# Second block of a two-block layer: pool products ahead of the gate branch's, gate branch kept in its banks, side taps by halves

## What is computed

```python
def second_block(x, meta_tokens, ...):
    h = concatenate([meta, x])
    u = rmsnorm(h, mix_norm_g)
    p = u @ w_in
    p_pool, p_bval, p_bgate, p_cgate, p_cx = split(p, [256, 256, 256, 512, 512])
    y_a = pool_mixer(p_pool, pool_w, pool_scale)        # running means of 2, 4, 8, 16, then a grouped product
    y_b = conformer_conv(p_bval, p_bgate, ...)          # 31 taps, layer norm, silu, product
    y_c = rglru_branch(p_cgate, p_cx, ...)              # 4 taps, gates, linear scan; gelu(p_cgate) * scan
    h = h + concatenate([y_a, y_b, y_c]) @ w_out
    u = rmsnorm(h, mlp_norm_g)
    h = h + square(relu(u @ w_up)) @ w_down
    return rmsnorm(h, final_norm_g)[16:]
```

## Time and profile before

| | us |
|---|---|
| median of 3 runs | 1053.14 (1053.1 to 1058.57) |
| the profiled execution | 1053.21 |
| its span | 1051.4 |
| PE busy | 1028.8 (98%) |
| DVE busy | 515.1 (49%) |
| ACT busy | 421.4 (40%) |
| POOL busy | 575.9 (55%) |

### The profile page before, as it was taken

How to read it: one execution, slowest core, us unless ns; L and a number is a source line. 1 busy time by engine, 2 the same in 40 slices (tenths; PEclk the granted TensorE clock), 3 DMA queues, 4 the chain that set the end, 5 groups by cost and what they waited for, 6 DMA issues and landing times.

```text
span 1051.4 us, 12703 instructions
## 1 busy us (share of the span) xinstructions
PE 1028.8 (98%) x5047; PEld 861.9 (82%) x5047; DVE 515.1 (49%) x835; ACT 421.4 (40%) x663; POOL 575.9 (55%) x712
## 2 busy tenths in 40 slices
PE   9999999999999999999999878999999999999997
PEld 7888888888888888888899766888788888888887
DVE  2781356665356633545677898457113213312323
ACT  5443445555624424443237663453213222212332
POOL 3655556556556764465634796464655544554551
PEclk9999999999999999999999999999999999999999
DMA  6323222122442215332222202322323232232212
GB/s 223 105 92 93 89 70 81 54 67 81 141 140 80 80 45 181 118 120 82 81 80 81 80 21 81 101 81 80 120 80 112 89 110 91 87 113 81 97 64 80
DMA packets 93500, 98.63 MB, mean 94 GB/s; under 512 B 3282, under 2 KB 88816, under 8 KB 93440
## 3 DMA queue, kind: packets, MB, share of 16 engines
q1 hardware_dynamic: 93440, 97.81, 28.7%
HBM read 95.71 MB, written 2.10 MB: 93 GB/s over the span
## 4 chain that ended last, share of the span: by engine, by line
PE 84%; DVE 11%; ACT 4%; issue 1%; DMA 1%; SPq 0%; DVEq 0%; ACTq 0%
PE ps L347 75%; DVE ps L1165 2%; PE ps L714 1%; PE ps L695 1%; PE ps L1623 1%; PE ps L839 1%; DVE Fm L1077 1%; DVE Hl L478 1%; PE ps L652 1%; PE ps L654 1%; DVE tmp L1589 1%; DVE Fm L1129 1%; DMA raw<-in_w_in 1%; DVE tmp L456 1%; DVE Al L1531 1%
## 5 line engine op out<-in xcount | busy, mean ns | idle before, releaser
L268 POOL TENSOR_TENSOR wlo<-raw,whi 128x256 fp32r<-128x256 f32 x668 | 509.4, 794 | 386.1 <-ACT whi L263 386.1
L347 PE MATMUL ps<-Hh,whi 128*128 128x512 f32 x832 | 330.0, 397 | 5.4 <-DVE Hl L1246 1.7
L347 PE MATMUL ps<-Hl,whi 128*128 128x512 f32 x832 | 325.4, 391 | 0.0
L263 ACT ACTIVATE whi<-raw 128x1024 fp32r<-128x1024 f32 x167 | 175.9, 1054 | 159.0 <-PE ps L347 152.7
L347 PE MATMUL ps<-Hh,wlo 128*128 128x512 f32 x832 | 209.1, 390 | 1.0 <-POOL wlo L268 1.0
L347 PE MATMUL ps<-Ah,whi 128*128 128x512 f32 (+1 forms) x576 | 197.7, 366 | 0.2 <-DVE Al L1531 0.2
L347 PE MATMUL ps<-Al,whi 128*128 128x512 f32 (+1 forms) x576 | 195.0, 361 | 0.0
L347 PEld LDWEIGHTS ps<-Hh,whi 128*128 128x128 f32 x832 | 156.9, 189 | 42.7 <-DVE Hl L408 4.2
L347 PEld LDWEIGHTS ps<-Hh,wlo 128*128 128x128 f32 x832 | 156.6, 188 | 34.2 <-POOL wlo L268 1.4
L347 PEld LDWEIGHTS ps<-Hl,whi 128*128 128x128 f32 x832 | 156.9, 189 | 31.8 <-issue 0.5
L347 PE MATMUL ps<-Ah,wlo 128*128 128x512 f32 (+1 forms) x576 | 125.2, 363 | 0.0
(11 more groups left out here) (291 smaller groups left out, 957.2 us busy)
## 6 DMA issues: line engine op xcount, KB each, us to landing
raw<-in_w_in SPq DMA_DIRECT2D x33, 1024.0 KB, 5.3
raw<-in_w_up SPq DMA_DIRECT2D x16, 1024.0 KB, 5.4
raw<-in_w_down SPq DMA_DIRECT2D x16, 1024.0 KB, 5.1
raw<-in_w_att_out SPq DMA_DIRECT2D x4, 1024.0 KB, 5.2
raw<-in_w_sg_out SPq DMA_DIRECT2D x4, 1024.0 KB, 5.2
raw<-in_w_o SPq DMA_DIRECT2D x4, 1024.0 KB, 5.1
raw<-in_w_in SPq DMA_DIRECT2D x6, 512.0 KB, 3.9
Fm<-in_x SPq DMA_DIRECT2D x2, 1024.0 KB, 6.7
```

The source lines that it names most:

```text
L263: eh = A(lambda e, s=s, src=src, kk=kk: e.activation(wtile(whi, s, kk), src, ACT.Copy), raw_ev[b], used)
L268: el = G(lambda e, s=s, src=src, kk=kk, cut=cut: e.tensor_tensor(wtile(wlo, s, kk)[:, *cut], src[:, *cut], f(wtile(whi, s, kk))[:, *cut], ...
L347: return e.matmul(ps[:, bk, 0:c1 - c0], wt, x[:, k, c0:c1], start=st, stop=sp)
```

## The change

- The two pool pair products move ahead of the four gate-branch products (and their weight columns in the load order).
- The first three gate-branch tiles stay in their banks: scale, gelu, product with the scan and both halves read and write `ps` (`at_cg`). Each bank is free for w_out when its low half is made. The fourth goes to SBUF as before.
- For each output half w_out takes the pool rows first, in all four banks, and then the rows of the gate branch.
- `x1_add` is split in two pairs, one behind each gate-branch product of the first half.
- `side_taps` becomes `side_tap(c)`, one half at a time; half 0 starts eight pieces earlier. Taps of half 0 move earlier too, many between `rg_high` and `rg_low`.
- `rg_conv(3)` to `rg_low(3)` move from the piece of gate(2,0), behind that gate, to the piece ahead of it; `rg_scan(1)` moves behind them.
- The pool pieces move with their products; `pool_high` is cut out of `pool_mix`.

```diff
+        cols("w_in_2", 0, 0, 1)
         cols("w_in_2", 0, 768, 2)
-        cols("w_in_2", 0, 0, 1)
         for i in range(2):
+            cols("w_out_2", 0, 512 * i, 1, 2, 1)
             cols("w_out_2", 512, 512 * i, 1, 4)
-            cols("w_out_2", 0, 512 * i, 1, 2, 1)
...
+        def side_tap(c):
+            k = side_at[c]
+            side_at[c] += 1
+            x = ub[:, c, k:k + 512]
+            s, fr = new_tmp()
+            dst = tmp[:, s, 0:512]
+            ea = A(lambda e: e.activation(dst, x, ACT.Copy, scale=cw[:, c, k:k + 1]), ub_ev[c], fr)
+            if k == N_DVE:
+                side_to[c], side_ev[c] = s, ea
+                return
+            acc = tmp[:, side_to[c], 0:512]
+            side_ev[c] = G(lambda e: e.tensor_tensor(acc, acc, dst, ALU.add), ea, side_ev[c])
+            release(s, side_ev[c])
...
+        def at_cg(c):
+            return ps[:, order4[c], :] if c < 3 else cg[:, c]
+
+        def scale_cg(c):
+            cg_ev[c] = scaled(at_cg(c), order4[c], Rb[:, 16:SM], cg_mm[c])
...
-                y2[4 + c] = [V(lambda e, c=c: e.tensor_tensor(Hl[:, 4 + c], cg[:, c], f(Hh[:, 4 + c]), ALU.subtract),
-                               cg_ev[c])]
+                ev = V(lambda e, c=c: e.tensor_tensor(Hl[:, 4 + c], at_cg(c), f(Hh[:, 4 + c]), ALU.subtract),
+                       cg_ev[c])
+                y2[4 + c] = [ev]
+                if c < 3:
+                    bank_free[order4[c]] = ev
...
+            side_tap(0)
             taps(4, (0,))
             yield
             cx(0, *made[2])
             taps(1, (0,))
             rg_conv(0)
             rg_high(0)
+            taps(1, (0,))
             rg_low(0)
+            side_tap(0)
             yield
             rescale(5, 6)
+            side_tap(0)
...
         for h in range(2):
+            product([[(bk, 0, 512)] for bk in order4], Hh, Hl, y2, (0, 1), 2, last=False, mid=step)
+            step()
             for g in range(2):
-                product([[(order4[2 * g], 0, 512)], [(order4[2 * g + 1], 0, 512)]], Hh, Hl, y2, range(4, 8), 4, last=False, mid=step)
+                rec_mm.extend(product([[(order4[2 * g], 0, 512)], [(order4[2 * g + 1], 0, 512)]], Hh, Hl, y2,
+                                      range(4, 8), 4, first=False, last=(h == 0), mid=step))
                 step()
-            evs = product([[(bk, 0, 512)] for bk in order4], Hh, Hl, y2, (0, 1), 2, first=False, last=(h == 0),
-                          mid=step)
-            if h == 0:
-                x1_add(0, evs)
-            step()
```

More of the change, by code:

```diff
@@ L1389, in mixers @@
+            taps(1, (0,))
             rg_conv(2)
             rg_high(2)
+            taps(1, (0,))
             rg_low(2)
             yield
-            side_taps()
-            taps(1, (1,))
+            side_tap(0)
+            side_tap(1)
             yield
             cx(3, *made[7])
-            taps(1)
+            side_tap(0)
+            taps(1, (1,))
+            rg_conv(3)
+            rg_high(3)
+            taps(1, (1,))
+            rg_low(3)
+            rg_scan(1)
             yield
@@ L1399, in mixers @@
             rg_gate(2, 0)
[L1400 to L1403, removed]
+            side_tap(1)
             yield
             rg_gate(2, 1)
-            scale_cg(0)
-            taps(1)
+            pool_in(0, *made[8])
+            side_tap(0)
+            rg_input(2)
             yield
             rg_gate(3, 0)
-            rg_input(2)
-            side_taps()
-            taps(1)
+            e3 = pool_mix(0)
+            side_tap(1)
             yield
@@ L1414, in mixers @@
             rg_gate(3, 1)
-            scale_cg(1)
-            rg_exps(2)
+            pool_in(1, *made[9])
+            ea = pool_high(0, e3)
+            rg_exps(2)
+            rg_input(3)
+            es = pool_low(0, ea)
+            yield
+            e3 = pool_mix(1)
+            side_tap(1)
+            rg_root(2)
+            table(ACT.Gelu_apprx_tanh)
+            ea = pool_high(1, e3)
+            yield
+            scale_cg(0)
+            es1 = pool_low(1, ea)
+            gelus((0,))
@@ L1417, in mixers @@
+            yield
+            e5 = pool_out(0, es)
+            side_tap(1)
+            rg_scan(2)
+            pool_out_low(0, e5)
+            yield
+            scale_cg(1)
+            gelus((1,))
+            side_tap(1)
+            cg_hi((0,))
+            rg_scan(3)
+            cg_lo((0,))
+            yield
+            cg_hi((1,))
+            side_tap(1)
             taps(1)
+            cg_lo((1,))
             yield
-            rg_input(3)
-            side_taps()
+            e5 = pool_out(1, es1)
@@ L1421, in mixers @@
+            scale_cg(2)
+            gelus((2,))
             taps(1)
-            yield
[L1423 to L1430, removed]
+            cg_hi((2,))
+            pool_out_low(1, e5)
+            taps(1)
+            cg_lo((2,))
+            side_tap(1)
+            yield
+            taps(3)
+            side_tap(1)
             yield
@@ L1433, in mixers @@
             gelus((3,))
[L1434 to L1452, removed]
             taps(1)
-            yield
+            cg_hi((3,))
             taps(1)
[L1456 to L1459, removed]
+            cg_lo((3,))
             yield
@@ L1464, in mixers @@
             yield
+            taps(3)
+            yield
+            x1_add((0, 1), rec_mm)
+            taps(3)
+            yield
+            taps(3)
+            yield
+            x1_add((2, 3), rec_mm)
             taps(N_DVE)
@@ L1486, in build @@
             step()
+        for i in range(2):
+            made.append(pair_product(mid=step))
+            step()
         order4 = (2, 3, 0, 1) if max(bank_age[0:2]) > max(bank_age[2:4]) else (0, 1, 2, 3)
```

56 lines of the change are left out of this document (20 added, 36 removed).

## The result

| | kernel before | changed kernel |
|---|---|---|
| median, us | 1056.31 (9 runs, 1052.78 to 1059.85) | 1049.07 (9 runs, 1046.85 to 1050.89) |
| profiled execution, its span | 1053.21, 1051.4 | 1048.39, 1046.2 |
| ratio | | 0.9936, 95% interval 0.9917 to 0.9954 |

A forecast was written before the change was run, and what follows sets the result against it. PE, busy 98%, bounds the kernel and loses 15.6 us between the first gate's stop and the layer-norm sums. Stops, first steps and clock afterwards sum to 10.4, so 5.2 is won: 1053.2 to 1048.0 us, range 1043.8 to 1053.0.

The forecast's parts named there:

- gate(1,0), behind rg_conv(1): PE near 562: new stop of 1.4 us, ended by ACT's sigmoid of gate(0,1); everything behind moves by it.
- gate(2,1), behind rg_conv(3): PE near 588 to 592: stop of 3.8 us in place of 2.23, since channel 3's L1081 precedes gate(2,0)'s sigmoid.
- L1256: Second pool tile's low part on DVE, done at 627.3; PE at the first w_out product's third step stops 3.4 us.
- fourth bank; last low half: PE behind L1256: waits for scale_cg(3) behind three taps, then for the gate branch's last Hl half; 0.45 us each.
- first steps behind stops: PE's first step behind each of five stops takes 0.08 us more, 0.4 in all.
- low clock: 0.4 us allowed for a PE clock fall; L1256's stop swallows up to 3.4 us of one behind the 3.8 stop.
- the road over ACT: From rg_root's result at 611.3: square root, table load of 1.28, pool_high, back to DVE at 613.9.
- Gate branch in its banks: Seven DVE operations get one tensor in a bank, priced 0.66 us to the next start; saves some 2.7 us of DVE.
- Taps and merge: Taps end and merge by 647.0, ACT's squares by 648.2, ahead of PE at 650; the merge's 1.12 us goes.
- Full blocking: 28 DVE operations between 578 and 627 cost 0.24 to 0.26 us more each; L1256 6.8 later; 1054.8 us; 11%.
- the meeting with more additions: POOL's thinner-spread side additions meet DVE's chain oftener, 0.53 us per operation; slower, about 1060 us; 8%.
- More won: POOL runs in DVE's gaps, L1256 precedes PE's need; the 3.4 us and 0.5 to 1 more go: 1044.0 us; 15%.

The follow-up runs named there:

- the side taps as before: Changed kernel with the side taps of both halves again together in nine pieces, from the scan of channel 0 on: median 1049.65 us.
- the last two versions: Changed kernel with gate(0,1) and gate(2,0) issued earlier, side taps and four DVE taps moved; then also L1241 before rg_root(2) and L1256 earlier: 1045.21 and 1042.41 us.
- the side taps away: Changed kernel with only side taps moved: half 0's last five to pieces from gate(1,0) on, half 1's, but for two, behind 620: median 1047.85 us.
- taps in the hole: Changed kernel with four DVE taps moved ahead of the second pool tile's L1244, where DVE waits 3.03 us for ACT's L1241: median 1048.01 us.

## Why the prediction was right, point by point

| term of the sum | forecast | measured |
|---|---|---|
| gate(1,0), behind rg_conv(1) | 1.4 | 1.48 |
| gate(2,0) | 0.15 | 0.19 |
| gate(2,1), behind rg_conv(3) | 3.8 | 3.65 |
| L1256 | 3.4 | 1.40 |
| fourth bank; last low half | 0.45; 0.45 | 0.16; 0.82 |
| first steps behind stops | 0.4 | some 0.5 (six) |
| low clock | 0.4 | 2.5 |
| sum | 10.4 | 10.7, and 0.8 in no stop |

The 0.8 is a term that the sum didn't have: idle counts from the end of a record of 0.40, but a step is 0.24, so a stop costs some 0.16 more than its idle, an estimate that gives 1.0 for the six.

- **The gates' stops.** Right in place, releaser and size. The chain was as written: three L1077, L1081, weight copy, sigmoid. The L1077 took 4.02 for 3.8 and 3.54 for 3.4.
- **What a fall of the clock costs.** Half right. The fall behind 591.17 took 2.5 us (15 steps in 6.28 us instead of 3.65, less 0.1 for the first). PE came to L1256 3.2 later than forecast and L1256 itself 1.2 later, so that the stop there was 1.40 instead of 3.4. Taking stop and fall away won 0.56 at L1256 and 0.25 at the sums. But the prediction said that the stop at L1256 swallows the fall, as if L1256 didn't depend on PE. It does by gate(3,1): PE ended that gate 49.5 behind the first stop instead of 47.2, and ACT's queue to L1241 begins there.
- **The stop at gate(1,0).** The prediction said that everything behind moves by it. That holds in part: with 0.9 of it gone, 0.3 was left at gate(2,0); with all of it gone, by the side taps as before, PE came 1.1 earlier at gate(2,1), and DVE's longer chain took it back.
- **L1256, the mis-sized term.** Forecast 74.0 behind the first stop (627.3 less 553.33), measured 75.2; nearly all of the 1.1 that the sums came later than forecast (97.2, 98.3). ACT and DVE there:

```profile
602.04 0.70 ACT L1095 ACTIVATE P<-ps,vec 128x528 f32<-128x528 f32 x1 [2.34 <-PE ps L1090]
...
604.52 1.28 ACT L1106 ACT_TABLE_LOAD   x1
...
609.84 1.28 ACT L1124 ACT_TABLE_LOAD   x1
611.13 0.65 ACT L1124 ACTIVATE Fm<-Fm 128x528 f32<-128x528 f32 x1
...
612.33 1.28 ACT L1325 ACT_TABLE_LOAD   x1
...
613.73 0.61 ACT L1241 ACTIVATE Hh<-Fm 128x512 fp32r<-128x512 f32 x1
```

```profile
601.31 0.71 DVE L1041 TENSOR_TENSOR Fm<-ps,Rb 128x528 f32<-128x528 f32 x1 [0.98 <-PE ps L347]
602.77 0.81 DVE L1115 TENSOR_TENSOR P<-P,Fm 128x528 f32<-128x528 f32 x1 [0.75 <-ACT P L1095]
603.50 1.79 DVE L1244 TENSOR_TENSOR Hl<-Fm,Hh 128x512 fp32r<-128x512 f32 x1
...
609.50 1.24 DVE L1120 SCALAR_TENSOR_TENSOR P<-Fm,P 128x528 f32<-128x528 f32 x1
...
614.38 0.69 DVE L1244 TENSOR_TENSOR Hl<-Fm,Hh 128x512 fp32r<-128x512 f32 x1 [3.03 <-ACT Hh L1241]
...
626.73 0.74 DVE L1256 SCALAR_TENSOR_TENSOR Hl<-ps,vec,Hh 128x512 fp32r<-128x512 f32 x1
```

  The step that failed is the road over ACT, 2.6 from rg_root's operand to DVE's L1244; it is 3.64 (610.74 to 614.38). I let ACT start when DVE's operand was there. But ACT has no gap from gate(3,1)'s sigmoid at 602.04 to L1241: exponentials, a weight copy, a side tap and three table loads of 1.28 stand in its own queue. So its length, begun by a late PE, set the hole; with L1241 ahead of the last two loads DVE's wait was gone. The rest: DVE's waits were 1.73, not 0.6, which puts its L1120 0.5 later; from L1244 to the end of L1256 it was 13.1 for 13.4.
- **Gate branch in its banks.** Price 0.66 to the next start, measured 0.60, records 0.66 to 0.69; undone it costs 2.9, forecast 2.7. By the diff six operations change, three L1196 and three L1203, not seven; five of them stand ahead of L1256.
- **Taps and merge.** The merge's stop of 1.12 went.
- **The rivals.** Full blocking (1054.8) and the meeting with more additions (1060) didn't come as sums: blocking is what the rows show (below), but in turns it costs the 1.13 and 1.66 that were counted. More won (1044.0) needed the chain shortened: it is what the last two versions do.
- **The base.** 1053.2 was one of the lower runs of before. A run of 1058.43 is 0.5 longer at the start, 1.6 at a clock of 0.98 between 300 and 400, 1.56 at gate(2,1) and 1.6 behind the sums. The medians' 7 us therefore hold more than the 4.1 of the stretch; how much of it the change did by leaving out stops, one trace doesn't settle. That the median came within 1.1 of the forecast is in part luck: the base was 3.1 below the median of the nine runs, and the gain of the medians was 7.2, not 5.2.

## What to carry to other kernels

Before you price a stop of the busy engine, find the last thing that it waits for behind it, and ask whether that thing's own chain starts on the busy engine, and where. A stop ahead of that start may be passed on whole, until another chain is the longer one: here the 2 us by which PE reached gate(3,1) earlier were worth 2.0 in one kernel, and 6 us were worth 0.25 in another. Follow the chain to that point through the queues of all engines, also where an engine seems to have time: what stands in its own queue (table loads, copies) can start the step later than its operand does. Where vector operations run beside another engine's, keep one tensor in a bank, and lay the other engine's work beside operations that have one there.

## What the runs showed of the hardware that I had not expected

**The length of a stop doesn't tell whether the clock falls.** The same stop of before at gate(2,1), 2.23 us both times, left the clock at 1.00 between 590 and 600 in the first trace and at 0.83 in the second, where one PE row behind it reads 0.63 for 0.39:

```profile
595.31 0.48 PE L1090 MATMUL ps<-Hh,M 128*128 128x264 f32 x2 [2.23 <-ACT Fm L1095]
...
596.93 0.63 PE L347 MATMUL ps<-Al,whi 128*128 128x512 f32 x1
```

With the side taps away a stop of 2.96 kept it at 1.00; with taps in the hole one of 2.23 at L1256 lowered it to 0.68 between 630 and 634. The length of a fall differs too: behind the same stop of 3.65 the way from gate(2,1) to gate(3,0) took 6.28 in the changed kernel and 5.03 with taps in the hole. And where a fall came with the stop at L1256, it cost next to nothing: the sums stayed 23.0 to 23.5 behind, since the two small stops that follow vanished.

**A contending pair overlaps less than I took from before.** POOL and DVE in the changed kernel:

```profile
632.17 1.31 POOL L1179 TENSOR_TENSOR tmp<-tmp 128x512 f32<-128x512 f32 x1
```

```profile
632.26 1.77 DVE L1196 TENSOR_TENSOR Fm<-Fm 128x512 f32<-128x512 f32 x1
```

The addition takes the time that it takes alone; DVE, begun 0.09 behind it, ends 0.55 after it. That is a full wait, and only some 0.1 of the 0.69 that such a record takes alone is hidden. The Trainium skill's SBUF — State Buffer, Who interferes with whom, says of DVE's 2-port modes that the engine which issues first gets the shared port pair for the whole instruction and the other fully blocks, and of a DVE instruction with two SBUF inputs that it contends with a GpSimd instruction that reads SBUF; this row agrees with both taken together. The 1.13 that I read as an overlap in part is the same in turns, as these rows of before show, POOL and then DVE:

```profile
631.40 1.19 POOL L268 TENSOR_TENSOR wlo<-raw,whi 128x256 fp32r<-128x256 f32 x1
```

```profile
632.04 1.12 DVE L1224 TENSOR_TENSOR tmp<-tmp 128x521 f32<-128x521 f32 x1
```

DVE ends 0.57 behind the weight part, and the part ends 0.59 behind DVE's operation before (at 632.00): together one turn of 1.16. So DVE meets only what POOL has to do then, and 0.5 to 1.1 us of it per operation, not all of it.
